# Neighbourhood attention on one core: the order of TensorE's steps per pair of heads

## What is computed

```python
s_loc = einsum('brqhd,brikhd->bhrqik', qg, kg) + bias[None]
s_ctx = einsum('brqhd,bchd->bhrqc', qg, kc)
p = softmax(concatenate([s_loc, s_ctx], axis=-1), axis=-1)
o = einsum('bhrqik,brikhd->brqhd', p_loc, vg) + einsum('bhrqc,bchd->brqhd', p_ctx, vc)
```

## Time and profile before

| | |
|---|---|
| median of 3 runs | 5323.18 us (5321.91 to 5332.97) |
| the profiled execution | 5320.74 us, span 5319.0 us |
| TensorE, matmuls | 4472.2 us busy (84%) |
| TensorE, weight loads | 3428.6 us busy (64%), beside the matmuls |
| VectorE | 2139.5 us busy (40%) |
| ScalarE | 1327.1 us busy (25%) |
| neighbourhood stage, layer 0 | about 966 to 1239 us |
| neighbourhood stage, layer 1 | about 2766 to 3020 us |

### The profile page before, as it was taken

One profiled execution on the slowest core, in us unless ns is written; L12 is line 12 of the kernel. 1 busy time (PEld: TensorE's weight loads), 2 busy tenths in 40 slices (PEclk: granted clock), 3 DMA queues, 4 the chain that ended last, 5 costly groups with the idle time before them and its releaser, 6 DMA issues. The chain is left out here.

```text
span 5319.0 us, 64375 instructions
## 1 busy us (share of the span) xinstructions
PE 4472.2 (84%) x25066; PEld 3428.6 (64%) x25066; DVE 2139.5 (40%) x4304; ACT 1327.1 (25%) x3110; POOL 424.6 (8%) x378
## 2 busy tenths in 40 slices
PE   5898997895867859989969866794999988969998
PEld 2787895673556727878847644583777766755555
DVE  3211011566456541110026656574480016655553
ACT  3000111464121030001126432113111126642222
POOL 1000001000001020000010000102240001100000
PEclk7999998997558979999989955796999999989999
DMA  4112116202105431121260210432112113342220
GB/s 167 60 65 82 60 59 193 85 13 85 44 14 195 160 137 68 66 79 71 91 198 14 72 44 21 159 139 112 60 58 81 62 65 123 95 173 88 88 88 24
DMA packets 200301, 472.77 MB, mean 89 GB/s; under 512 B 41016, under 2 KB 96568, under 8 KB 186748
## 3 DMA queue, kind: packets, MB, share of 16 engines
q1 hardware_dynamic: 191168, 437.99, 23.5%
q0 software_dynamic: 8832, 30.68, 1.5%
HBM read 308.42 MB, written 160.19 MB: 88 GB/s over the span
## 5 line engine op out<-in xcount | busy, mean ns | idle before, releaser
L72 PE MATMUL tm_tacc<-tm_tw_hi,hT_hi 128*128 128x384 f32 (+1 forms) x1120 | 409.7, 366 | 40.9 <-DVE tm_tw_lo L407 31.0
L73 PE MATMUL tm_tacc<-tm_tw_lo,hT_hi 128*128 128x384 f32 (+1 forms) x1120 | 405.9, 362 | 0.0
L74 PE MATMUL tm_tacc<-tm_tw_hi,hT_lo 128*128 128x384 f32 (+1 forms) x1120 | 405.9, 362 | 0.0
L72 PE MATMUL tz_tacc<-tz_tw_hi,hT_hi 128*128 128x512 f32 x896 | 360.3, 402 | 37.0 <-DVE tz_tw_lo L407 24.8
L72 PE MATMUL cm_acc<-hT_hi,cm_wb_hi 128*128 128x512 f32 (+1 forms) x912 | 342.0, 375 | 20.2 <-DVE cm_wb_lo L317 20.2
L73 PE MATMUL tz_tacc<-tz_tw_lo,hT_hi 128*128 128x512 f32 x896 | 356.7, 398 | 0.0
L74 PE MATMUL tz_tacc<-tz_tw_hi,hT_lo 128*128 128x512 f32 x896 | 356.5, 398 | 0.0
L73 PE MATMUL cm_acc<-hT_lo,cm_wb_hi 128*128 128x512 f32 (+1 forms) x912 | 341.6, 375 | 0.0
L74 PE MATMUL cm_acc<-hT_hi,cm_wb_lo 128*128 128x512 f32 (+1 forms) x912 | 341.4, 374 | 0.0
L72 PEld LDWEIGHTS tm_tacc<-tm_tw_hi,hT_hi 128*128 128x128 f32 x1120 | 211.1, 188 | 75.6 <-DVE tm_tw_lo L407 35.8
L404 DVE CAST tm_tw_hi<-tm_traw 128x512 fp32r<-128x512 f32 (+1 forms) x64 | 48.8, 762 | 513.0 <-PE tm_tacc L74 477.6
(11 more groups left out here) (300 smaller groups left out, 8593.4 us busy)
## 6 DMA issues: line engine op xcount, KB each, us to landing
scr_z<-tz_tz SPq DMA_DIRECT2D x112, 256.0 KB, 2.0
ada_w<-in_w_ada SPq DMA_DIRECT2D x16, 1536.0 KB, 18.3
scr_zcm<-cm_zo SPq DMA_DIRECT2D x18, 1152.0 KB, 5.1
scr_ztm<-tm_tz SPq DMA_DIRECT2D x68, 256.0 KB, 2.0
out_mx<-scr_mix SPq DMA_DIRECT2D x34, 512.0 KB, 4.6
out_gt<-scr_ztm SPq DMA_DIRECT2D x34, 512.0 KB, 5.5
scr_xres<-out_x POOLq DMA_DIRECT2D x34, 512.0 KB, 2.9
nt_xb<-scr_xres SPq DMA_DIRECT2D x8, 2048.0 KB, 10.3
```

Of the source, the lines that this page charges most:

```text
L72: nc.tensor.matmul(out, ah, bh, start=start, stop=False)
L73: nc.tensor.matmul(out, ah, bl, start=False, stop=False)
L74: return nc.tensor.matmul(out, al, bh, start=False, stop=stop)
```

## The change

In TensorE's loop the step `values(p - 1)`, with the waits that guard its first execution, stands right behind the scores and ahead of the first transposes. The other engines' programs are the same.

```diff
                 for p in range(NP + 2):
                     if p + 1 < NP:
                         score_pair(p + 1)
-                    if p < NP:
-                        transposes(2 * p)
-                    if p >= 2:
-                        back(p - 2)
                     if p == 1:
                         pe.wait_ge(v_in, 16)
                         pe.wait_ge(pz_ok, 1)
                     if 1 <= p <= NP:
                         values(p - 1)
+                    if p < NP:
+                        transposes(2 * p)
+                    if p >= 2:
+                        back(p - 2)
                     if p < NP:
                         transposes(2 * p + 1)
```

## The result

| | median | runs | profiled execution |
|---|---|---|---|
| before | 5323.58 us | 4 (5321.91 to 5332.97) | 5320.74 us, span 5319.0 |
| after | 5381.45 us | 4 (5374.25 to 5385.93) | 5384.98 us, span 5383.2 |

The ratio is 1.0104, with a 95% interval of 1.0086 to 1.0121: the change makes the kernel 57.9 us slower. The forecast was 5377, some 54 us more than before.

A forecast was written before the change was run, and what follows sets the result against it. TensorE's own queue was taken to bound inner pairs, VectorE's queue border pairs. Losses of 33.3, 12.5, 5.3, 1.5 and 1.0 make 53.6 us: 5323.2 + 53.6 = 5377 us, own range 5361 to 5394, 8-in-10 range 5350 to 5402.

The forecast's parts named there:

- The values find their inputs ready: Values in their new place, right behind the scores, were to wait for nothing, with at least half a microsecond to spare.
- The unknown step from scores to values: Start-to-start time on TensorE not shown in the trace; taken as 1.71 us, with ends 0.16 less and 0.17 more.
- TensorE's way: Inner pair: second transposes wait for VectorE's copy (4.08), start at 4.91, next scores at 5.82 us.
- VectorE's way: Inner pair: the next maximum, queued behind VectorE's copy, starts at 4.68 and lets the next scores start at 5.79 us.
- The border periods: Pairs of the two row tiles at either image end: 5.57 us against 4.74, 0.83 more, bound by VectorE's chain.
- The sum: Total loss over all periods of both layers' neighbourhood stages: 53.6 us, with ends 38 and 71.
- inner periods: Scores to scores in pairs between the border tiles: 5.82 us against 5.33, 0.49 more, 68 times, 33.3 us.
- the eight at the seams: Periods between border and inner tiles, with steps of both kinds: 0.66 us more each, 5.3 us together.
- The five context periods: Layer 0's periods with context queries: one wait for ScalarE's copy goes, a like one arises; 0.3 us each, 1.5 together.
- The ends of the two loops: The drain at the end of each layer's loop, unrolled once in the new order: 0.5 us each, 1.0 together.
- The gain by one change of kind less: Rival: three changes of matmul kind a pair, not four, with waits hidden, save about 0.16 us each; 5311 us; chance 5%.
- The clock: Rival: new idles on TensorE lower its clock in a tenth of the periods, 33 us on top, 5410 us; chance 8%.

The follow-up runs named there:

- maxima first: Changed kernel with VectorE's order per pair made maximum, maximum, copy, copy, and a fourth buffer of s: 5381.63 us, ratio 1.0108.
- half of the change: Against the kernel before, values moved ahead of the back transpose but not ahead of the first transposes: 5324.62 us, ratio 1.0001.
- the extra copy: One more VectorE copy of tpa ahead of every even unit's copy: 5423.87 us in the changed kernel, 5340.38 us in the kernel before.

## Why the prediction was right

**The values find their inputs ready: right.** They start 1.72 behind the scores, without a wait on their inputs (forecast 1.71). The unknown step from scores to values cost what scores to transposes had cost; neither end of its bound was needed.

**TensorE's way: right.** Copy at 4.09 (forecast 4.08), second transposes at 4.93 (4.91), scores at 5.81 (5.82). With maxima first this way stands alone, at 5.81.

**VectorE's way: right, 0.02 too long.** With two `tpa` banks it stands alone at 5.77 (forecast 5.79). The estimate of about 0.1 from the maximum's end to the scores was 0.07: 1.08 from its start, of which the operation is 1.01.

**The border periods: right.** 5.58 against 5.57, on VectorE's way.

**The sum.** 68 inner periods grew by 32.4 us together (forecast 33.3), the 15 border periods by 12.7 (12.5), the eight at the seams, 0.48 to 0.91 each, by 5.5 (5.3). The five context periods grew from 3.92, 3.32 and three times 2.43 to 4.40, 3.56 and three times 2.68: 1.5, as forecast. The ends of the two loops grew by 0.7 and 1.3, 2.0 in all, where 1.0 had been put down: in layer 1 the last values wait 0.85 and 0.56 for VectorE's copies, where before only the very last waited, 0.46. Layer 0's very first period took 6.45 instead of 5.16. No values stand in it, and its steps are the same before and after; what differs is the clock, granted 0.62 over the stage's first 14 us before and 0.50 in the changed kernel, and the same 0.50 in the kernel with half of the change. So these 1.3 are not the order's. Together 55.3, where 53.6 was forecast.

**What was luck.** That the median came within 5 us of the forecast owes something to chance. The range was 33 us wide, and the phases outside the two stages moved by up to 19 us from one execution to another, which its sum put at nothing. The mechanism is shown by the periods and stages, not by the whole time.

**The rivals.** The gain by one change of kind less did not come in the changed kernel, and the point from which it was said to decide was the right one: the copy must be done when the back transpose is. Once the waits were opened it came, 0.15 a pair against the 0.16 that this rival had named. The clock stayed at 1.00 with 171.98 of 186 us busy, 92%, as in the two stretches that spoke against that rival. The Trainium skill ("TensorE: Matmul & The Clock Gate", section "A second HAM failure mode: psum-queue depth-cycling") tells of a bf16 kernel in which short idles between groups of matmuls made the clock go up and down. The changed kernel's even stretch doesn't show that, with an idle of 0.44 us in every 5.81 and a granted 1.00.

**What was off.** In the study, not in the prediction: the border period of the run with maxima first, expected at 5.28 and measured at 5.61. The walk had moved the second maximum ahead of the copy without moving the copy behind it. And several whole times fell outside what was expected, while all other periods came within 0.1 us of it: whole times of this kernel carry the spread of the other phases.

## What to carry to other kernels

A long matmul step between two uses of a single-buffered PSUM bank is the cover of the copy that empties it. Before moving such a step, walk one period through every engine's queue: what is queued behind the copy (here the next maximum) can be a second chain of the same length, and then removing either wait alone buys next to nothing. If all the waits that the step covered are opened, the order that was bad can be the better one.

## What the runs showed of the hardware

- One change of kind less per pair on TensorE (64-row scores, full transposes, 64-column values) saved 0.15 us here: 5.33 with four changes a period and 5.18 with three, with the same work and no idle. The Trainium skill says that changing the tiling mode drains TensorE ("TensorEngine Tiling (Array Packing)", section "Key Properties"). The trace agrees in so far as a change costs time; that a drain is the reason, no run here shows.
- VectorE's next operation starts before the last one's recorded end: 0.60 from start to start behind a copy of 0.69 (1063.38 and 1063.98 in the earlier trace rows), so 0.60 is what a copy in the chain costs, as the extra copy did.
- Phases with the same code took 4779 to 4798 us together in the twelve profiled executions, so effects of 0.1% were read from periods and stages, not from the whole time.
